# Where the tiles of a decoder layer start inside a partition, and the way by which its bias vectors reach DRAM

## What is computed

```
x = x + 0.5 * swiglu_ffn(rmsnorm(x, ffn1_norm), ffn1_w_in, ffn1_w_out)      # D_FF = 5504
h = rmsnorm(x, mix_norm)
qa, ka, va, qb, kb, vb, f_pre = split(h @ w_in)
out_a = dilated_attention(rmsnorm(qa), rmsnorm(ka), va, rel_bias_table)     # 8 heads
out_b = forgetting_attention(rmsnorm(qb), rmsnorm(kb), vb, log_sigmoid(f_pre + forget_bias))   # 8 heads
x = x + concat(out_a, out_b) @ w_out
x = x + 0.5 * swiglu_ffn(rmsnorm(x, ffn2_norm), ffn2_w_in, ffn2_w_out)
```

## The kernel before

| tile | start before | mod 1024 | mod 256 | start after |
|---|---|---|---|---|
| x | 16,512 | 128 | 128 | 17,408 |
| xs | 32,896 | 128 | 128 | 33,792 |
| raw | 65,664 | 128 | 128 | 66,560 |
| whi | 90,240 | 128 | 128 | 91,136 |
| wlo | 106,624 | 128 | 128 | 107,520 |
| act, mix | 138,944 | 704 | 192 | 140,288 |

## Time and profile before

### The profile page before, as it was taken

One profiled execution on the slowest core, in us unless ns is written; L12 is line 12 of the kernel. 1 busy time (PEld: TensorE's weight loads), 2 busy tenths in 40 slices (PEclk: granted clock), 3 DMA queues, 4 the chain that ended last, 5 costly groups with the idle time before them and its releaser, 6 DMA issues.

```text
span 1929.6 us, 20375 instructions
## 1 busy us (share of the span) xinstructions
PE 1880.1 (97%) x8470; PEld 1549.7 (80%) x8470; DVE 946.6 (49%) x1051; ACT 818.1 (42%) x971; POOL 27.0 (1%) x36
## 2 busy tenths in 40 slices
PE   6799999999999999999999999999999999999999
PEld 5588888888988888877777777888888888988887
DVE  4355454544545454356555555544554444544443
ACT  5244444444434443344445445444444444433332
POOL 1000000000000000000000000000000000000000
PEclk9999999999999999899999999999999999999999
DMA  6665555555555555444544545555555555555553
GB/s 217 142 200 188 184 195 193 183 191 180 193 189 181 186 189 200 147 146 138 163 165 153 172 156 170 181 194 194 178 195 192 183 192 186 188 188 202 199 193 110
DMA packets 176171, 347.12 MB, mean 180 GB/s; under 512 B 6128, under 2 KB 14376, under 8 KB 176080
## 3 DMA queue, kind: packets, MB, share of 16 engines
q1 hardware_dynamic: 172304, 337.92, 52.7%
q0 software_dynamic: 1696, 3.96, 1.1%
q10 hardware_dynamic: 2080, 3.94, 0.6%
HBM read 342.13 MB, written 3.67 MB: 179 GB/s over the span
## 4 chain that ended last, share of the span: by engine, by line
PE 92%; DVE 3%; DMA 2%; ACT 2%; issue 1%; ACTq 0%; DVEq 0%
PE acc L244 29%; PE acc L246 29%; PE acc L245 29%; ACT whi L454 2%; DMA raw<-ffn_w_in 2%; DVE wlo L672 1%; PE aux L271 1%; DMA x<-x 1%; PE aux L261 1%; PE aux L323 0%; PE aux L374 0%; PE aux L366 0%; PE aux L384 0%; PE aux L365 0%; PE aux L336 0%
## 5 line engine op out<-in xcount | busy, mean ns | idle before, releaser
L672 DVE TENSOR_TENSOR wlo<-raw,whi 128x1024 fp32r<-128x1024 f32 (+1 forms) x656 | 790.4, 1206 | 948.0 <-ACT whi L454 947.1
L454 ACT ACTIVATE whi<-raw 128x1024 fp32r<-128x1024 f32 (+1 forms) x656 | 684.7, 1045 | 1071.2 <-PE acc L246 1048.8
L244 PE MATMUL acc<-whi,xs 128*128 128x512 f32 (+1 forms) x1792 | 701.9, 392 | 17.1 <-DVE wlo L672 17.1
L246 PE MATMUL acc<-whi,xs 128*128 128x512 f32 (+1 forms) x1792 | 693.9, 387 | 0.0
L245 PE MATMUL acc<-wlo,xs 128*128 128x512 f32 (+1 forms) x1792 | 693.5, 387 | 0.0
L244 PEld LDWEIGHTS acc<-whi,xs 128*128 128x128 f32 x1792 | 338.6, 189 | 82.8 <-DVE wlo L672 14.0
L246 PEld LDWEIGHTS acc<-whi,xs 128*128 128x128 f32 x1792 | 338.2, 189 | 66.5
L245 PEld LDWEIGHTS acc<-wlo,xs 128*128 128x128 f32 x1792 | 338.6, 189 | 64.1
L244 PE MATMUL acc<-whi,act 128*128 128x512 f32 x688 | 272.5, 396 | 0.0
L245 PE MATMUL acc<-wlo,act 128*128 128x512 f32 x688 | 272.1, 395 | 0.0
L246 PE MATMUL acc<-whi,act 128*128 128x512 f32 x688 | 272.1, 395 | 0.0
(11 more groups left out here) (115 smaller groups left out, 522.0 us busy)
## 6 DMA issues: line engine op xcount, KB each, us to landing
raw<-ffn_w_in SPq DMA_DIRECT2D x160, 1024.0 KB, 5.0
raw<-ffn_w_out SPq DMA_DIRECT2D x80, 1024.0 KB, 5.0
raw<-w_in SPq DMA_DIRECT2D x48, 1024.0 KB, 5.1
raw<-w_out SPq DMA_DIRECT2D x16, 1024.0 KB, 5.0
raw<-ffn_w_in SPq DMA_DIRECT2D x16, 768.0 KB, 4.4
raw<-ffn_w_out SPq DMA_DIRECT2D x8, 768.0 KB, 4.3
x<-x ACTq DMA_DIRECT2D x4, 512.0 KB, 13.4
bias_vectors<-vec POOLq DMA_DIRECT2D x1, 1536.0 KB, 34.9
```

Source lines behind the costliest of these rows:

```text
L244: mm(banks[b][:, 0:w], stationary[:, k, 0, tok], hi, start=k == 0, stop=False, skip_group_check=True)
L246: last = mm(banks[b][:, 0:w], stationary[:, k, 1, tok], hi, start=False, stop=k == k_total - 1, skip_group_check=True)
L454: A(whi[:, h % SLOTS, 0:n_el], raw[:, slot, first:first + n_el], ACT.Copy).then_inc(weights_hi, 1)
L672: V.tensor_tensor(wlo[:, h % SLOTS, 0:n_el], raw[:, slot, first:first + n_el], whi[:, h % SLOTS, 0:n_el].bitcast(f32), ALU.subtract).then_ ...
```

## The change

Three things. The running place starts at a multiple of 1024 instead of 64. The arena starts at a multiple of 1024 too. And the bias vectors take another way: one transfer writes them to DRAM once, as one row of 3072 values; when it has landed, a second copies that row within DRAM to 128 rows. The later reads into `dmat` wait for the second, and have the same shapes with other steps. All large tiles keep their sizes and their distances from each other up to `junk`; the arena lies 448 bytes further from them.

```diff
-        place = [-(-nc.sbuf_base // 64) * 64]
+        place = [-(-nc.sbuf_base // 1024) * 1024]
...
         f_bias = sb("f_bias", [P, H_B])
+        place[0] = -(-place[0] // 1024) * 1024
         arena = place[0]
...
-        scratch = nc.dram_tensor("bias_vectors", (H_A, P, VEC), f32).ap()
+        vec_dram = nc.dram_tensor("bias_vector", (1, H_A * VEC), f32).ap()
+        scratch = nc.dram_tensor("bias_vectors", (P, H_A * VEC), f32).ap()
...
             pool.wait_ge(vec_ready, 1)
-            pool.dma_start(scratch, vec[:].rearrange("h (a v) -> h a v", a=1).to_broadcast([H_A, P, VEC])).then_inc(vec_stored, 16)
+            pool.dma_start(vec_dram.rearrange("a (h v) -> (a h) v", h=H_A), vec[:]).then_inc(vec_stored, 16)
+            pool.wait_ge(vec_stored, 16)
+            pool.dma_start(scratch, vec_dram.to_broadcast([P, H_A * VEC])).then_inc(vec_copied, 16)
             pool.wait_ge(weights_used, QKV)
-            pool.wait_ge(vec_stored, 16)
+            pool.wait_ge(vec_copied, 16)
...
             for b in range(TB):
                 src = bass.AP(tensor=scratch.tensor, offset=SEQ - 1 - b * P,
-                              ap=[[VEC - 1, P], [P * VEC, H_A], [1, (b + 1) * P]])
+                              ap=[[H_A * VEC - 1, P], [VEC, H_A], [1, (b + 1) * P]])
```

More of the change, by code:

```diff
@@ L129, in layer @@
         x_loaded = [sem(f"x_loaded{c}") for c in range(N_OUT)]
-        gains_loaded, gains2_loaded, f_loaded, vec_loaded, mixer_loaded, vec_stored = (
-            sem(n) for n in ("gains_loaded", "gains2_loaded", "f_loaded", "vec_loaded", "mixer_loaded", "vec_stored"))
+        gains_loaded, gains2_loaded, f_loaded, vec_loaded, mixer_loaded, vec_stored, vec_copied = (
+            sem(n) for n in ("gains_loaded", "gains2_loaded", "f_loaded", "vec_loaded", "mixer_loaded", "vec_stored", "vec_copied"))
         small_set, ident_zero, ident_ready, table_warm = (sem(n) for n in ("small_set", "ident_zero", "ident_ready", "table_warm"))
```

## The result

The changed kernel takes 1898.53 us in the median of 4 runs (1896.87 to 1902.12), the kernel before in the same comparison 1930.73 (1929.42 to 1932.72): a ratio of 0.9835, 95% interval 0.9817 to 0.9853. That is 32 us faster where 113 were forecast, at the far end of the range of 1798 to 1900. The time is that of the first rival, "only the difference goes", which said 1898; whether its cause is right too is what most of the experiments are about.

What follows compares the result with a forecast made beforehand. PE's matmul pace and one long standstill were taken to bound the kernel. From the median 1930.03 us, 16.2 us for the standstill and 96.7 us net for tile starts were subtracted, giving 1817 us, range 1798 to 1900.

Steps and rivals of the forecast that it cites:

- the first rival: Large matmuls: only the further 6.7 ns on `act` and `mix` goes, 16.3 us, 13.3 ns stay; 1898 us, chance 0.24.
- The bound and the pace: Whole kernel: PE busy 97% of the span; 512-column matmuls take 226.6 ns on `xs`, 233.3 on `act`.
- The stop: PE starts nothing from 81.74 to 95.72 us, weights delayed by the bias-vector transfer; removal, slow clock included, gains 16.2 us.
- the cover of 12 us: Mixer's projection near the new copy: weight pieces can come some 12 us late before PE stands still.
- The starts: All 7824 large matmuls: tiles at multiples of 1024 avoid bytes fetched in vain; net gain 96.7 us.
- the sum's term of 101.7 us: Large matmuls, before deductions: 58.6 us gained on `xs` plus 43.1 us on `act` and `mix`.
- The prediction's own sign: Profile after: the forecast is wrong altogether if the pace gets better only on one of the operands.
- PE's own cost per instruction: Aligned large matmuls: 2.4 ns over the columns, taken from transposes at 108.8 ns, so 215.7 ns at 512 columns.
- slower: Large matmuls: an aligned start counts as a full 256 bytes, 26.7 ns surplus; 2002 us, chance 0.05.
- The grown waits: Mixer: 27 waits of PE for chains through DVE each grow about 0.15 us as halves shorten, 4 us lost.
- the starts don't matter: Large matmuls: 6.7 ns comes from the tile's place or distance from `whi`; only 16.2 us go, 1913.8 us, chance 0.07.

Runs made afterwards that it cites:

- the scan: Changed kernel with `xs`, `act` and `mix` moved 32 to 448 bytes past multiples of 1024, moving tiles at multiples of 1024; three runs: 1947.59, 1933.43 and 1908.53 us.

## Why the prediction was wrong

**The bound and the pace** were read rightly: the time is PE's, at 226.7 and 233.3 ns per matmul of 512 columns.

**The stop** was right in cause and size. 16.2 us forecast, 16.7 us measured for that part alone. The copy was sized at 4.5 us of delay; the piece beside it came 5.6 us late, and that was within the cover of 12 us. How far the cover reaches, no run tried.

**The starts** were wrong, at the step "both surpluses are what is fetched in vain if reads begin at the multiple of 256 below the start". Two points, 128 bytes for 13.3 ns and 192 for 20.0, lay on a line through zero at PE's own 9.6 bytes per ns, and I took the fit for a mechanism. In both points the distance to `whi` changed with the start, 0 and 64, and I weighed that only in half a sentence of a rival. Worse, that rival had the stop alone go, as if the change kept the distance; but the arena moves 448 bytes further from `whi`, and 64 + 448 is 512, in step within 256. The runs put two separate things in its place: some 13.3 ns for each matmul with its weight load, which no placement moved, and a toll of up to 7.6 ns when the two operands don't start in step within 256 bytes. The change removed the toll from 2448 matmuls, 2448 x 6.67 = 16.3 us by the rival's sum, 15.3 measured for that part alone. Of the sum's term of 101.7 us, the 58.6 us on `xs` were not there at all, and of the 43.1 us on `act` and `mix` 15.3 were. The prediction's own sign came: the pace got better on one of the operands only. The first rival had the split of the surplus and the time right; its cause for the 6.7 ns, the start of `act` by itself, was wrong, so its 1898 is in part luck.

**The warning was in the rows.** Transposes of 128 columns at 108.8 ns let me set PE's own cost per instruction at 2.4 ns. They stream at one column in two cycles; nothing there shows what a stream at full pace costs beside a weight load. The bound from above, 13.3 ns that stay, stood in the text as a rival at 0.24 and should have had the larger share. Two smaller slips changed nothing: the rival "slower" decides from a surplus of 17.5 ns, (16.2 + 71.7 + 49.0) us over 7824 matmuls, not 16 to 17; and before 34 us there are 49 large matmuls, not about 90.

**The grown waits** (4 us) were not put to the test: with `xs` unchanged the halves of the mixer's projection got no shorter, and it kept its length, 339.6 and 339.2 us.

**The rival "the starts don't matter"**, which the lines of 16 bytes in the Trainium skill's "SBUF — State Buffer" ("Specifications (TRN2)") would also give, is refuted as far as distances go: 32 bytes of distance cost 6.7 ns. That an aligned start as such brings nothing agrees with it.

## What to carry to other kernels

Two points on a line through zero are no mechanism when a second quantity moved along with the first; look which operand pairs were in step before pricing an alignment, and keep the full surplus as the bound for what may stay. Place the stationary and the moving operand of dense fp32r matmuls at the same offset within 256 bytes; 0, 64 and 128 did equally well here, and no distance was tried with another format. And a broadcast out of a few partitions is slow for the transfers beside it, not only for itself: the pieces of weights beside it took 26 to 31 us instead of 5. With the vectors written once and then copied within DRAM they took at most 11.

## What the runs showed that I had not expected

- The distance between the starts of a matmul's two operands bears on its pace, alike at 0 and 256 and at 192 and 448 bytes: with the moving tiles at multiples of 256, 0 costs nothing, 192 costs 2.3 ns on average, other multiples of 32 between 5.7 and 7.6 ns.
- Moving both by 64 bytes costs nothing. Moving the moving tiles alone, by 64 and 128, costs 5.5 ns, more than their distance within 256 gives by the scan and less than its bare size gives.
- With weight loads of 64 columns instead of 128 the stream beside them was slower, 230.1 ns for 226.8.
- 13.3 ns per matmul stay at 256, 384 and 512 columns, and 11.8 with bf16 views, at 2.4 GHz; at 1.2 GHz nothing is over (seven matmuls).
- A copy of 1.5 MB from one row of DRAM to 128 rows landed in 9.0 us while the weights flowed beside it; from 60 to 75 us the two made 314 GB/s.
